# Two one-pass products of a high and a low half in place of one fp32 product, for the sums of the attended values' squares

## The reference

```
def rms_norm(x, g):
    y = xf * lax.rsqrt(jnp.mean(xf * xf, axis=-1, keepdims=True) + EPS)
    return y * g
...
def mixer_out(o_attn, o_rec, subln, lam_init, w_out):
    oa = (rms_norm(o_attn, subln) * (1.0 - lam_init)).reshape(B, T, ATTN_WIDTH)
    return jnp.concatenate([oa, o_rec], axis=-1) @ w_out
```

## Time and profile before

| | |
|---|---|
| median of 3 executions | 1529.02 us (1528.67 to 1530.77) |
| profiled execution, its own time | 1528.63 us |
| its span (first to last instruction) | 1526.8 us |
| mean granted clock of TensorE in it | 0.985 of full speed |
| PE busy | 1484.9 us, 97% of the span |
| DVE busy | 946.0 us, 62% |
| ACT busy | 496.2 us, 32% |
| POOL busy | 442.8 us, 29% |

### The profile page before, as it was taken

The page is one execution under the profiler, slowest core; times in us unless marked ns, Lnnn a source line. Parts: engine busy times, 40 slices in busy tenths (PEclk is TensorE's granted clock), DMA queues, the critical chain, the costliest instruction groups (busy, mean ns, idle before and its releaser), DMA issues.

```text
span 1526.8 us, 24430 instructions
## 1 busy us (share of the span) xinstructions
PE 1484.9 (97%) x9601; PEld 1410.5 (92%) x9601; DVE 946.0 (62%) x1548; ACT 496.2 (32%) x992; POOL 442.8 (29%) x210
## 2 busy tenths in 40 slices
PE   7999999999999998999999999999999999999998
PEld 5888988898889887689999999999999999999998
DVE  6458545755665477674666657475756666574755
ACT  6537445645654564363411101010101011010111
POOL 0000300120021003230372717263452717272520
PEclk8999999999999999999999999999999999999999
DMA  8221003102200215453021111021101011120102
GB/s 280 87 56 42 28 17 98 42 28 63 80 16 27 72 43 157 152 180 102 1 84 57 29 56 61 23 81 31 56 28 56 28 56 33 50 69 26 58 0 114
DMA packets 124591, 97.90 MB, mean 64 GB/s; under 512 B 4615, under 2 KB 114572, under 8 KB 124524
## 3 DMA queue, kind: packets, MB, share of 16 engines
q1 hardware_dynamic: 123566, 96.72, 20.4%
q10 hardware_dynamic: 958, 0.26, 0.1%
HBM read 77.45 MB, written 19.52 MB: 64 GB/s over the span
## 4 chain that ended last, share of the span: by engine, by line
PE 57%; issue 0%; ACT 0%; DVE 0%; ACTq 0%; DVEq 0%
PE f_gp L143 6%; PE f_up L143 6%; PE f_gp L145 6%; PE f_gp L144 6%; PE f_dn L2154 6%; PE f_up L144 5%; PE f_up L145 5%; PE f_dn L2155 5%; PE f_dn L2156 5%; PE f_up L2056 2%; PE f_up L2057 2%; PE f_up L2058 2%; PE f_gp L2185 0%; PE f_up L2185 0%; PE f_gp L2089 0%; PE f_dn L2123 0%
## 5 line engine op out<-in xcount | busy, mean ns | idle before, releaser
L135 POOL TENSOR_TENSOR m_hi<-m_raw,ones 128x1024 fp32r<-128x1024 f32 x66 | 163.5, 2477 | 447.0 <-PE f_gp L145 271.4
L2467 DVE TENSOR_TENSOR room<-room,f_dn 128x352 f32<-128x352 f32 x264 | 137.6, 521 | 117.0 <-PE f_dn L2156 117.0
L143 PE MATMUL z_ps<-h_hi,w_hi 128*128 128x352 f32 x600 | 203.6, 339 | 0.0
L145 PE MATMUL z_ps<-h_hi,w_lo 128*128 128x352 f32 x600 | 195.8, 326 | 0.0
L144 PE MATMUL z_ps<-h_lo,w_hi 128*128 128x352 f32 x600 | 195.3, 325 | 0.0
L136 POOL TENSOR_TENSOR m_lo<-m_raw,m_hi 128x1024 fp32r<-128x1024 f32 x66 | 186.0, 2819 | 5.2
L143 PE MATMUL f_gp<-f_hi,m_hi 128*128 128x352 f32 x528 | 172.4, 327 | 0.5 <-DVE room L2346 0.5
L2154 PE MATMUL f_dn<-f_ahi,m_hi 128*128 128x352 f32 x528 | 171.6, 325 | 0.9 <-DVE room L2467 0.9
L143 PE MATMUL f_up<-f_hi,m_hi 128*128 128x352 f32 x528 | 170.3, 323 | 0.0
L2155 PE MATMUL f_dn<-f_alo,m_hi 128*128 128x352 f32 x528 | 169.9, 322 | 0.0
L2156 PE MATMUL f_dn<-f_ahi,m_lo 128*128 128x352 f32 x528 | 169.9, 322 | 0.0
(11 more groups left out here) (325 smaller groups left out, 3174.1 us busy)
## 6 DMA issues: line engine op xcount, KB each, us to landing
w_raw<-w_in SPq DMA_DIRECT2D x28, 512.0 KB, 3.9
m_raw<-w_gate SPq DMA_DIRECT2D x22, 512.0 KB, 3.9
m_raw<-w_up SPq DMA_DIRECT2D x22, 512.0 KB, 3.9
m_raw<-w_down SPq DMA_DIRECT2D x22, 512.0 KB, 5.2
room<-x_d SPq DMA_DIRECT2D x3, 1408.0 KB, 7.7
room<-x_prompt SPq DMA_DIRECT2D x8, 512.0 KB, 7.3
s_kp<-cache_k SPq DMA_DIRECT2D x16, 256.0 KB, 3.0
m_raw<-w_out SPq DMA_DIRECT2D x8, 512.0 KB, 5.3
```

The source lines that it names most:

```text
L135: link(nc.gpsimd.tensor_tensor(hi, raw, ones.rearrange("p (o c) -> p o c", o=1).broadcast_to(list(raw.shape)), ALU.mult))
L143: nc.tensor.matmul(out, whi[:, k, :], hi[:, k, :], start=(k == 0), stop=False)
L145: last = nc.tensor.matmul(out, wlo[:, k, :], hi[:, k, :], start=False, stop=(k == chunks - 1))
L2467: v.tensor_tensor(acc[:, d, piece(n)], acc[:, d, piece(n)], dn[b][:, 0:PW], ALU.add).then_inc(dn_free[b], 1)
```

## The change

The squares are split into a high and a low half, and each half of the columns gets two products with a tile of ones of type F32R, summed in PSUM, in place of one fp32 product. ACT makes the squares twice: once in fp32 (S1) and once into an F32R tile `sq_hi`; DVE subtracts (`square_low`) and writes `sq_lo` over S1. The tile of ones is exact in one half, so no low half of it is needed. `ones_r` is copied once at the start. `sq_hi` lies in the space of the X tile that level 4 used, which is why ACT waits for level 4's product.

```
+        sq_hi = at("sq_hi", [P, T], 19424 + 3 * TT, F32R)
+        sq_lo = at("sq_lo", [P, T], 5472, F32R)
+        ones_r = sb("ones_r", [P, P], F32R)
...
+        sqh_ready = sem("sqh_ready")
...
 def attention_squares(h):            # PE
-                        mm(bank, keep["ones"][:, :], S1[:, 512 * half:512 * half + 512], start=True, stop=True).then_inc(rec_ready[u % 2], 1)
+                        cols = slice(512 * half, 512 * half + 512)
+                        mm(bank, ones_r[:, :], sq_hi[:, cols], start=True, stop=False)
+                        mm(bank, ones_r[:, :], sq_lo[:, cols], start=False, stop=True).then_inc(rec_ready[u % 2], 1)
...
 def attention_square(h):             # ACT
                     act.wait_ge(tb_free, tb_use(h, "p7"))
-                    a(S1[:, 0:T], OA, ACT.Square).then_inc(sqa_ready, 1)
+                    a(S1[:, 0:T], OA, ACT.Square)
+                    act.wait_ge(rec_ready[L_USE[4] % 2], rec_use(h, L_USE[4]))
+                    a(sq_hi[:, :], OA, ACT.Square).then_inc(sqh_ready, 1)
...
+                def square_low(h):   # DVE
+                    dve.wait_ge(sqh_ready, h + 1)
+                    v.tensor_tensor(sq_lo[:, :], S1[:, 0:T], sq_hi[:, :].bitcast(F32), ALU.subtract).then_inc(sqa_ready, 1)
...
 def recurrence(h):                   # DVE
                     level(h, 6)
+                    square_low(h)
                     level(h, 7)
                     sample_updates(h)
...
 def last_recurrence(h):              # DVE
                     turned_weights(1)
+                    square_low(h)
                     sample_attended(0)
                     sample_updates(h)
...
-                v.memset(keep["ones"][:, :], 1.0)
+                link(v.memset(keep["ones"][:, :], 1.0))
+                v.tensor_copy(ones_r[:, :], keep["ones"][:, :])
```

## The result

The changed kernel takes 1537.15 us in the median of 20 executions (1529.77 to 1539.33); the kernel before, timed with it, 1531.54 us (1519.91 to 1534.33). The ratio is 1.0046, interval 1.003 to 1.0063: slower by nearly half a per cent, where no change was forecast (1528.8, range 1526.2 to 1531.8). The profiled execution took 1536.21 us, with a span of 1534.4 and a mean granted clock of 0.980; that of the kernel before had 1526.8 and 0.985.

The account below looks back on a forecast made before the run. PE, 97% busy, was taken to bound the kernel. Heads 0 to 2 gain 1.4 us and the last head loses 1.2, so -0.2 us: 1528.4 on the profiled execution, 1528.8 as median, range 1526.2 to 1531.8.

Parts of the forecast that it names:

- the bank order: At the sums of squares: both halves wait for DVE's sample updates, so only the second half stands in PE's way.
- The rival of the whole saving: All four heads: each gives back most of its roughly 2 us, 3.4 us in all, 1525.6 us; chance 0.09.
- the products and head 1: Second half of the sums: 0.61 us in place of 1.05; head 1 gains 0.34 us after a 0.10 us delay.
- the 1.4: Heads 0 to 2 together gain 1.4 us: 0.48 in head 0, 0.34 in head 1, 0.60 in head 2.
- the hold in the last head: Last head: DVE's subtraction waits for POOL's first low half and ends 1.1 us after it; `sample_attended(0)` starts 1.7 us late.
- The path's loss: Last head: the delayed subtraction makes the sums end later, 1.2 us lost; bounds 0.7 and 3.5 us.
- the clock, in its chance and in its price: Rival: fewer passes bring the lower clock in head 1 and the last head too, 1.7 us each, 1532.2 us; chance 0.12.
- the last head's term: Last head: the late subtraction pushes the updates and sums, 1.2 us lost.
- the fall was taken to keep its length: Heads 0 and 2: work moved into the won time runs at half clock, leaving 0.48 us of head 0's 0.95.
- The rival's own picture: Clock rival: head 0's lower clock comes in head 1 and the last head as well, staying where it was; chance 0.12.
- The prediction's own sign of being wrong: Whole kernel: the prediction is wrong if the granted clock falls in more than one place where it did not before.

Follow-up runs that it names:

- e3: Against the kernel before: one-pass products alone, ACT writing the square once, no subtraction, both products taking the high half; 1529.55 us, ratio 0.9993.
- e4: Against the changed kernel: the last head's subtraction moved ahead of the turned weights' copies on VectorE; 1533.07 us, ratio 1.0008 to the kernel before.
- e10: Against the changed kernel: filler products that nobody reads in PE's waits at the last head's sums alone; 1530.71 us, ratio 0.9989 to the kernel before.
- e7: Against the kernel before: the change in heads 0 to 2 alone, the last head keeping the fp32 product; 1528.80 us, ratio 0.9987.
- e8: Against the kernel before: the change in the last head alone, heads 0 to 2 as they were; 1537.47 us, ratio 1.0034.
- e1: The kernel before, unchanged, run to have the granted clock beside each execution's time; 1531.14 us, ratio 1.0001.
- e6: Against the changed kernel: heads 0 to 2's sums behind the next head's first scores and transposes, last head's subtraction earlier; 1530.10 us, ratio 0.9993 to the kernel before.
- e2: Against the changed kernel: its waits and subtraction kept, but one fp32 product per half, of the high half alone; 1533.63 us, ratio 1.0016 to the kernel before.
- e5: Against the changed kernel: filler products that nobody reads in PE's waits at the sums of all four heads; 1527.51 us, ratio 0.9979 to the kernel before.
- e9: Against the kernel before: only filler products that nobody reads, in PE's waits at the sums of all four heads; 1527.81 us, ratio 0.9977.
- e12: Against the kernel before: the change in heads 0 to 2 alone, plus filler products in all four heads' waits; 1526.69 us, ratio 0.9958.

## Why the prediction was wrong

**Right: the bank order.** L782 still waits for DVE's L1565, 6.6 us in eleven waits, those of PE and of its weight load counted apart. The rival of the whole saving is refuted by e3, 0.6 us of level for 3.4.

**Right: the products and head 1.** 0.61 us were forecast from the second half's start to the next scores, and 0.66 measured (361.31 to 361.97); the sample updates were to end 0.2 us later, and with 2.33 in place of 2.05 us their length alone makes it 0.28; 0.34 us were to be won, and 0.31 were. The two products of a half start 0.31 to 0.34 us apart and not 0.23, 0.1 us mis-sized, yet the scores follow nearly when they were reckoned to. With the clock's part taken out, heads 0 to 2 gave 1.1 us for 1.4. How near these two are is partly luck: the 1.4 had two heads priced at the lower clock, and three times head 1's 0.34 would be 1.0.

**Right: the hold in the last head.** `square_low` takes 1.22 to 1.23 us in three heads and 1.79 in the last. POOL's first low half runs from 639.61 to 641.97; the subtraction, begun at 641.26, ends at 643.05, 1.08 us later, for 1.1 forecast. POOL's second starts at 641.94 and takes 3.32 in place of 2.36 us, so it waited as well. The Trainium skill's rule (SBUF — State Buffer, "SBUF: two separate sides"), that one of the two stands still for the other's whole instruction, agrees with this case in both directions. In e4, where the subtraction starts ahead of POOL, it takes 1.23 us again. The path's loss was to be 1.2 us and is 1.27, by e10 and e7.

**Wrong: the clock, in its chance and in its price.** Three steps of the prediction treated it too lightly. "With half the passes PE does less around the sums" got a chance of 0.12, when the same text had shown that the clock in head 0 hung by little. The step that failed is the last head's term: its lateness was priced as its own length, 1.2 us, and the clock behind it stood in the sum with nothing. The lateness is made of a wait of 2.17 us on PE, and behind that wait the clock fell through the second half of the sums and the two groups of products behind it (L832 and L836), for 3.17 us more. And in heads 0 and 2 the fall was taken to keep its length, with half of the won time left at its end; in the profile after a second fall follows instead, 3.5 x (0.48 + 0.49) = 3.4 us not granted in place of 1.7. That this costs anything in the average isn't shown: e7 has none of it. The rival's own picture, a fall in head 1 and one in the last head, was half off: head 1 had none, and the one ahead of it was gone. What decided was one place, the last head: of the 7.3 us more not granted, e8 has 5.5 by itself and e7 none (each uncertain by 3 to 4), and the filler there takes back all (21.9). The prediction's own sign of being wrong, falls in more than one place where there had been none, came in the profile.

Was it the wait, or the fewer passes? The fourteen profiles, from the last head's sums to the last product of the first block, are of four kinds. With the old products and a wait of 0.48 us (before, e1, e7) the clock stays up. With the new products and the same wait of 0.48 (e3, e4, e6) it falls once, through L836: 3.42, 3.55 and 3.49 us where it was 1.92. Behind the long wait (after, e2, e8) it falls earlier and stays down twice as long, with old and new products alike. With the filler (e5, e9 to e12) it stays up. L836 in e3_passes_only, then in e6_behind:

```profile
648.00 3.42 PE L836 MATMUL S<-s_kp,s_PT 128*32 128x512 f32 x16
...
639.50 3.49 PE L836 MATMUL S<-s_kp,s_PT 128*32 128x512 f32 x16
```

So both count there, the wait for more. The single fall can't be seen in the averages of e3, e4 and e6 (22.0, 24.7 and 21.8 us not granted against 22.9).

The Trainium skill's rule quoted in the prediction (TensorE: Matmul & The Clock Gate, "What's actually happening"), the lower clock as the default that activity lifts, gives the sign. The trace agrees with it here: filler products, which do nothing but keep PE active, brought the clock back. That fewer passes by themselves bring the lower clock more often, as the prediction drew from it, the averages don't show: e3 has 22.0 us not granted against 22.9.

**Open.** The rows show 3.4 us not granted at 645 to 653 of the changed kernel; e8's average says 5.5. The fall behind, at 659 to 663, adds nothing, since the kernel before has its like at 653 to 656.5. Places before the last head show single falls in one profile and double ones in another for the same code (345.5 to 349.5 in the kernel before, 347.5 to 355 in e8_last_only), so part of an average from twelve executions is such scatter. Why a microsecond not granted costs 0.71 and not 1, I didn't isolate.

## What to carry to other kernels

Price a wait on TensorE by what the clock does behind it as well as by its length: look at the granted clock of the stretch after each wait that a change lengthens, and at the length of a known product there (here 2.07 against 1.12 us). When a change moves a kernel by a few microseconds, compare the clock that wasn't granted before looking for a longer path. If a wait can't be removed, products into a spare bank that nobody reads can be worth more than they cost, and a kernel with them is the fair base for judging the change itself.

## What the runs showed that I had not expected

The time of an execution follows the mean granted clock closely, whatever the kernel: 0.71 us for each microsecond not granted, over clocks from 0.977 to 0.993, with 0.9 us of scatter. The unchanged kernel alone ranges from 0.981 to 0.992 and from 1520 to 1536 us.

A fall can come behind thin work and land on dense work. Stretches of e5_fill in head 0, to be held against those of the kernel after: the same scores and transposes, with the filler in e5's wait ahead of them. PE has 3.50 of 3.50 us busy in both (219.00 on, above), at 0.51 there and at 1.00 here. That the filler made the difference in this place isn't shown: in e7's profile, with the same products and no filler, the clock is at 1.00 here too.

```profile
216.00:219.50 3.50, 3.50 (x23) 2.94 (x22) 2.94 (x10) 0.37 (x1) 0.00 (x0) 1.00 0.01 2
219.50:223.00 3.50, 3.50 (x29) 2.93 (x28) 1.08 (x4) 3.46 (x4) 0.00 (x0) 1.00 0.00 0
```
